# Ring slots, one-hot buffers and row counts in the expert stage of a diffusion trunk step

## What is computed

```python
q = einsum('btd,dhk->bthk', h, w_query).reshape(B, T, 8, 2, 128)
s = einsum('bthpk,hpnk->bthpn', q, sub_keys)     # 128 scores for each of two half keys
sv, si = top_k(s, 16)
best, pos = top_k(all 256 sums of a pair, 16)    # 16 of 16384 experts for each head
gates = softmax(best)
act = gelu(einsum('nd,ned->ne', h, expert_u[idx]))
out = einsum('ne,ned->nd', act * gates, expert_v[idx])
x = x + gt2 * out ; y = rmsnorm(x, norm_final)
```

## Time and profile before

| | |
|---|---|
| median of 3 runs | 5057.17 us (5048.15 to 5059.45) |
| the profiled execution, whole | 5038.0 us |
| its span in the trace | 5036.2 us |
| PE busy | 4752.4 us, 94% of the span |
| DVE busy | 3017.1 us, 60% |
| POOL busy | 1775.7 us, 35% |
| ACT busy | 579.1 us, 11% |
| mean granted clock of PE, as a share of full speed | 0.968 |
| read from HBM | 1643.31 MB, 330 GB/s over the span |
| the four stretches of the expert stage | from 3224.15 to 5023.83 us in the trace |

### The profile page before, as it was taken

The page is one execution under the profiler, slowest core; times in us unless marked ns, Lnnn a source line. Parts: engine busy times, 40 slices in busy tenths (PEclk is TensorE's granted clock), DMA queues, the critical chain, the costliest instruction groups (busy, mean ns, idle before and its releaser), DMA issues.

```text
span 5036.2 us, 54841 instructions
## 1 busy us (share of the span) xinstructions
PE 4752.4 (94%) x22501; PEld 3559.3 (71%) x22501; DVE 3017.1 (60%) x4381; ACT 579.1 (11%) x1078; POOL 1775.7 (35%) x1113
## 2 busy tenths in 40 slices
PE   4989999998999999899999999999999989999998
PEld 1787446445999444347555445799999988998898
DVE  1441006897766777317777578878855457776444
ACT  1521001441222100000000001100000000000000
POOL 0131001674555565211544353333432333332221
PEclk7999999999999999999999999999999999999999
DMA  9919898995221998996999987599999998999997
GB/s 389 380 51 351 314 342 323 386 392 233 76 89 68 371 396 342 414 352 255 420 420 420 376 346 294 205 372 406 409 407 405 397 381 346 353 347 363 377 366 302
DMA packets 262301, 1666.68 MB, mean 331 GB/s; under 512 B 28274, under 2 KB 32770, under 8 KB 78660
## 3 DMA queue, kind: packets, MB, share of 16 engines
q0 software_dynamic: 130048, 939.72, 46.7%
q1 hardware_dynamic: 123460, 673.84, 34.8%
q10 hardware_dynamic: 8544, 49.62, 2.5%
HBM read 1643.31 MB, written 18.94 MB: 330 GB/s over the span
## 4 chain that ended last, share of the span: by engine, by line
PE 33%; DMA 13%; DVE 7%; issue 2%; POOL 1%; ACT 0%; ACTq 0%; DVEq 0%; POOLq 0%
PE ps L241 14%; PE ps L2296 11%; DMA arena_sb<-peer_u,arena_sb 7%; DMA arena_sb<-peer_v 5%; PE ps L1720 4%; PE ps L2239 2%; DMA arena_sb<-peer_v,arena_sb 2%; DVE arena_sb L400 2%; DVE arena_sb L395 1%; DVE arena_sb L2486 1%; POOL arena_sb L349 0%; DVE arena_sb L2002 0%; DVE arena_sb L2012 0%; DVE arena_sb L2004 0%; DVE arena_sb L1999 0%
## 5 line engine op out<-in xcount | busy, mean ns | idle before, releaser
L241 PE MATMUL ps<-arena_sb 128*128 128x224 f32 (+3 forms) x9728 | 2317.9, 399 | 5.7 <-PEq L552 3.7
L241 PEld LDWEIGHTS ps<-arena_sb 128*128 128x128 f32 x9728 | 1692.8, 194 | 624.7 <-issue 336.4
L400 DVE SCALAR_TENSOR_TENSOR arena_sb<-arena_sb 128x2048 f32<-128x2048 f32 x412 | 985.8, 2393 | 397.7 <-DMA arena_sb<-peer_v,arena_sb 378.9
L395 DVE CUSTOM_DVE_ANT_0 arena_sb<-arena_sb 128x2048 f32<-128x2048 f32 x416 | 962.0, 2332 | 302.7 <-DMA arena_sb<-peer_u,arena_sb 302.5
L349 POOL DMA_INDIRECT arena_sb<-peer_v,arena_sb x416 | 688.3, 1655 | 1097.3 <-DVE arena_sb L400 579.0
L349 POOL DMA_INDIRECT arena_sb<-peer_u,arena_sb x416 | 654.8, 1574 | 851.1 <-DVE arena_sb L395 403.5
L2296 PE MATMUL ps<-arena_sb 128*128 128x224 f32 x4096 | 790.0, 355 | 33.7 <-DMA arena_sb<-peer_v 32.3
L2296 PEld LDWEIGHTS ps<-arena_sb 128*128 128x128 f32 x4096 | 776.8, 191 | 45.9 <-DMA arena_sb<-peer_v 42.4
L1570 PE MATMUL ps<-arena_sb 128*128 128x512 f32 x768 | 343.1, 605 | 20.9 <-PEq L2603 7.8
L1570 PEld LDWEIGHTS ps<-arena_sb 128*128 128x128 f32 x768 | 146.0, 193 | 213.4 <-issue 195.8
L1720 PE MATMUL ps<-arena_sb 128*128 128x512 f32 x640 | 277.9, 596 | 16.1 <-DVE arena_sb L1501 12.3
(11 more groups left out here) (279 smaller groups left out, 2919.7 us busy)
## 6 DMA issues: line engine op xcount, KB each, us to landing
arena_sb<-peer_ut SPq DMA_DIRECT2D x128, 1024.0 KB
arena_sb<-peer_v SPq DMA_DIRECT2D x128, 1024.0 KB
arena_sb<-w_mod POOLq DMA_DIRECT2D x64, 1024.0 KB, 9.0
arena_sb<-w_qkv SPq DMA_DIRECT2D x48, 1024.0 KB
arena_sb<-w_out SPq DMA_DIRECT2D x48, 1024.0 KB
arena_sb<-w_query SPq DMA_DIRECT2D x48, 1024.0 KB
arena_sb<-w_mod SPq DMA_DIRECT2D x32, 1024.0 KB
arena_sb<-w_ga_r SPq DMA_DIRECT2D x32, 1024.0 KB
```

The source lines that it names most:

```text
L241: mm = pe.matmul(out, weights[:, k * P:(k + 1) * P], x[:, k, :], start=(k == 0), stop=(k == chunks - 1))
L395: nc.vector.tensor_tensor_reduce(rows, rows, total, 1.0, 0.0, ALU.mult, ALU.add, seg.dots[:, p:p + 1]).then_inc(t.rows_used, 1)
L400: nc.vector.scalar_tensor_tensor(out=total, in0=rows, scalar=seg.weight[:, p:p + 1], in1=total, op0=ALU.mult, op1=ALU.add).then_inc(t.rows ...
```

## The change

Five edits in `experts`:

1. The second one-hot buffer moves from the scratch area to columns of `r.h2t` that the dense way doesn't read (tokens 224 and up), and both buffers are now used in both halves (`i = g % 2`).
2. In u1 `hot` stands two tiles ahead of its matmuls instead of one, and in both halves it stands before `use_rows` of its tile instead of after. In u1 the first `hot` also waits until all v tiles of half 0 are done, since `ring[3]` holds one of them.
3. `ring[3]` takes v tiles: a table `slot_of` cycles through slots 3, 1, 2, 0 in v0 and 3, 2, 0, 1 in v1, and through three slots in u0 and u1. A load waits until the tile before it in its slot is done. The first v load of a half also waits for the last group of gate matmuls.
4. `counts` moves row steps. By the two lists u0 has 100 instead of 98, v0 83 instead of 89, u1 122 instead of 112, and v1 has what remains of 374: 69 instead of 75. The first row step stands at tile 7 instead of 8.
5. x of the second segment no longer lies in `ring[3]` but shares a buffer with the first, so its load and what follows from it come some tiles later (tile 12 instead of 9 for `combine(1)`). The loads of `gt` and `norm` wait for the last gate matmuls, since they now overwrite the second one-hot buffer.

```diff
-    full = [t.sem(f"ex_full{i}") for i in range(3)]
+    full = [t.sem(f"ex_full{i}") for i in range(4)]
...
-    hots = ring[3], t.m[:, C + 8192:C + 8192 + TILE]
-    weighted = [ap[:, 0:TOKENS * P].rearrange("p (u n) -> p u n", u=TOKENS) for ap in hots]
-    plain = [ap[:, TOKENS * P:TOKENS * (P + HALF)].rearrange("p (u n) -> p u n", u=TOKENS) for ap in hots]
+    weighted = [ring[3][:, 0:TOKENS * P].rearrange("p (u n) -> p u n", u=TOKENS),
+                r.h2t[:, 0:TOKENS, DENSE:DENSE + P]]
+    plain = [ring[3][:, TOKENS * P:TOKENS * (P + HALF)].rearrange("p (u n) -> p u n", u=TOKENS),
+             r.h2t[:, TOKENS:2 * TOKENS, DENSE:DENSE + HALF]]
...
-    x = [t.m[:, DD + 2 * D:DD + 3 * D], ring[3], t.m[:, DD + 2 * D:DD + 3 * D], lead.total, spare.total]
+    x = [t.m[:, DD + 2 * D:DD + 3 * D], t.m[:, DD + 2 * D:DD + 3 * D], t.m[:, DD + 2 * D:DD + 3 * D], lead.total, spare.total]
...
+    slot_of, fill, before, last_in, fills = [], [], [], [None] * 4, [0] * 4
+    for cycle in ((0, 1, 2), (3, 1, 2, 0), (1, 2, 0), (3, 2, 0, 1)):
+        for i in range(HALF):
+            s = cycle[i % len(cycle)]
+            fills[s] += 1
+            slot_of.append(s)
+            fill.append(fills[s])
+            before.append(last_in[s])
+            last_in[s] = len(slot_of) - 1
...
-    hot_after = [{}, {s - 1: [g] for s, g in group_at[1].items()}]
-    for g, s in enumerate(starts[0]):
-        hot_after[0].setdefault(max(s - 2, starts[0][0] - 1), []).append(g)
+    hot_after = [{}, {}]
+    for h in range(2):
+        for g, s in enumerate(starts[h]):
+            hot_after[h].setdefault(max(s - 2, starts[h][0] - 1), []).append(g)
...
-    counts = [0] * 8 + [2, 2, 2, 1] * 14 + [1, 2, 1, 1, 2] * 12 + [1, 2, 1, 1] + [2, 1, 2, 2] * 16 + [1] + [1, 2, 1, 1] * 15
+    counts = [0] * 7 + [2, 2, 2, 1] * 14 + [2] + [1, 1, 2, 1, 1, 2, 1, 1, 2, 1] * 6 + [1, 1, 2, 1] + [2, 2, 2, 2, 2, 2, 2, 2, 2, 1] * 6 + [2] * 4 + [1, 1, 1, 1, 2] * 12
...
-            else:
-                sp.wait_ge(tile, n - 2)
+            elif before[n] is not None:
+                sp.wait_ge(tile, before[n] + 1)
+            if n % (2 * HALF) == HALF:
+                sp.wait_ge(gate_ps, GROUPS * (n // (2 * HALF) + 1))
...
-            n, i = GROUPS * h + g, 0 if h else g % 2
-            if h:
-                dve.wait_ge(gate_ps, n)
-            elif n > 1:
+            n, i = GROUPS * h + g, g % 2
+            if h and g == 0:
+                dve.wait_ge(tile, 2 * HALF)
+            if n > 1:
                 dve.wait_ge(gate_ps, n - 1)
...
                 gate(h, s)
-                use_rows(dve, nc, t, behind[2 * HALF * h + s])
                 for g in hot_after[h].get(s, ()):
                     hot(h, g)
+                use_rows(dve, nc, t, behind[2 * HALF * h + s])
```

More of the change, by code:

```diff
@@ L2184, in _ @@
                 sp.wait_ge(t.tile_done, base - 3 + n)
-            else:
-                sp.wait_ge(tile, n - 2)
+            elif before[n] is not None:
+                sp.wait_ge(tile, before[n] + 1)
+            if n % (2 * HALF) == HALF:
+                sp.wait_ge(gate_ps, GROUPS * (n // (2 * HALF) + 1))
             h, v = n // (2 * HALF), n % HALF
             if n // HALF % 2 == 0:
-                sp.dma_start(ring[n % 3], a["peer_ut"][HALF * h + v]).then_inc(full[n % 3], 16)
+                sp.dma_start(ring[slot_of[n]], a["peer_ut"][HALF * h + v]).then_inc(full[slot_of[n]], 16)
             else:
@@ L2193, in _ @@
                 low = (HALF * h + u * v) * P
-                sp.dma_start(ring[n % 3].rearrange("p (u n) -> p u n", u=u),
+                sp.dma_start(ring[slot_of[n]].rearrange("p (u n) -> p u n", u=u),
                              a["peer_v"][low:low + u * P, c * P:(c + w) * P]
-                             .rearrange("(u p) n -> p u n", u=u)).then_inc(full[n % 3], 16)
+                             .rearrange("(u p) n -> p u n", u=u)).then_inc(full[slot_of[n]], 16)
         for i, (out, n) in enumerate(dense):
@@ L2216, in loaded @@
         def loaded(n):
-            pe.wait_ge(full[n % 3], 16 * (n // 3 + 1))
+            pe.wait_ge(full[slot_of[n]], 16 * fill[n])
         def turn_keys():
@@ L2295, in add_rows @@
                         col = (s % u * w + i) * P
-                        mm = pe.matmul(t.ps[:, bank_of[h][first + i], 0:DENSE], ring[(n - 1) % 3][:, col:col + P],
+                        mm = pe.matmul(t.ps[:, bank_of[h][first + i], 0:DENSE], ring[slot_of[n - 1]][:, col:col + P],
                                        acts[:, s, :], start=(s == 0 and h == 0), stop=(s == HALF - 1))
@@ L2314, in _ @@
                 loaded(n)
-                project(pe, t.ps[:, u_banks[h][s % 2], 0:DENSE], ring[n % 3], h2t).then_inc(tile, 1)
+                project(pe, t.ps[:, u_banks[h][s % 2], 0:DENSE], ring[slot_of[n]], h2t).then_inc(tile, 1)
                 if h == 0 and s == starts[0][0] - 2:
@@ L2427, in _ @@
             if h:
+                act.wait_ge(gate_ps, 2 * GROUPS)
                 act.wait_ge(t.x_spilled, 16 * (2 * NB - 1))
@@ L2431, in _ @@
                 load_x(0)
-                act.wait_ge(gate_ps, 2 * GROUPS)
-                load_x(1)
             for s in range(HALF):
@@ L2437, in _ @@
                 if h:
[L2438 to L2443, removed]
+                    if s in (5, 12):
+                        square(s // 12)
+                    if s in (7, 14):
+                        store(s // 14)
+                    if s in (6, 13):
+                        load_x(1 + s // 13)
                     if s == 15:
@@ L2551, in _ @@
                 if h:
[L2552 to L2555, removed]
+                    if s in (5, 12):
+                        combine(s // 12)
+                    if s in (6, 13):
+                        scale(s // 13)
                     if s == 54:
```

## The result

| | kernel before | changed kernel |
|---|---|---|
| median of 4 runs | 5052.66 us | 4969.61 us (4955.71 to 4971.03) |
| ratio, 95% interval | 1 | 0.9835 (0.9802 to 0.9868) |
| span of the profiled execution | 5036.2 us | 4967.6 us |

The gain is 83 us where 86 were forecast. The windows of the changed kernel show where it lies. The columns are those of the earlier trace rows, and so are the stretches: u0, v0, u1, and v1 in two parts.

What follows compares the result with a forecast made beforehand. PE was taken to be held by waits for DVE's one-hot matrices in u1, with its lower clock, and for v tiles in v0 and v1. Gains 5 + 54 + 10 + 17 = 86 us off 5057.17 gave 4971 us, range 4948 to 5015.

Steps and rivals of the forecast that it cites:

- u1: the work of DVE ahead of PE: u1: PE waits for one-hot matrices behind DVE's row steps; 77.3 us lost, 35.5 in waits, 41.8 at PE's lower level.
- The floor: u1 without waits: 64 tiles with 28 groups are 437.3 us, plus one sum of 5.5 us, 442.8 us.
- u1: DMA becomes the limit: u1: 195.0 MB make DMA the new limit; 464 us at 420 GB/s, 483 at 404; taken as 466, gain 54.
- The first rival: u1: DMA gives what is asked, up to 440 GB/s; u1 443 to 455 us, kernel 4945 to 4960; chance 0.12.
- the fourth (354 GB/s): u1: DMA already at its limit of 354 GB/s; u1 551 us, kernel 5056, no change; chance 0.03.
- u1: "the first wait stays": Start of u1: PE's first wait, 7.74 us, stays, since group 0 has ten row steps ahead of it before and now.
- The second rival: u1: late gathers hold DVE and the next `hot`, the clock stays lower; kernel 4988 to 5025; chance 0.27.
- v0: the step that failed: v0: 147 blocks at 401 GB/s are 384 us, below PE's 389.8, so PE bounds; 394 us, gain 10.
- v1: the term that was mis-sized: v1: fewer row steps and a fourth slot shorten the two long waits; gain 17 us, bounds 6 and 26.
- u0: u0: `hot` ahead of row steps removes one wait of 2.54 us and its slow matmuls; gain 5, bound 0 to 8.
- The third rival: u0 and u1: row steps behind `hot` free slots 2.9 us later and starve the queues; kernel at 5136; chance 0.05.
- The sum: Whole kernel: 5 + 54 + 10 + 17 = 86 us off the median, 4971 us.

Runs made afterwards that it cites:

- half tiles: Changed kernel loading only the first half of the columns of each u tile of half 1, output no longer the reference's: 4940.3 us in one run.
- rows first: Changed kernel with `use_rows` moved back ahead of `hot`, still two tiles ahead: 4987.87 us, ratio 0.9875.

## Why the prediction was right, and where it was not

**u1: the work of DVE ahead of PE.** Right. With edits 1 and 2 alone all the loss goes, waits and slow clock together. The floor was set 1.8 us too high: the row of 5.51 us in the earlier trace rows stands behind a wait, at the lower clock, and in a u1 without waits this sum adds 3.7 us to a pair of tiles. So u1 lost 79 us, not 77.3.

**u1: DMA becomes the limit.** Right, and the main term of the sum: 461.8 us against 466. Its two rates were 404 and 420 GB/s; the trace shows 413 at a share of 1.00. The two kernels that change only bytes settle it: 6 steps more cost 14 us, and half the tile bytes bring the floor. The first rival (440 GB/s) and the fourth (354 GB/s) fall with it. That 466 came so near is partly luck: all 195.0 MB at 413 GB/s would take 472 us, and u1 was shorter because it left part of its bytes to v1, which the sum didn't have. By the Trainium skill's rule of about 358 GB/s (page "DMA: Bandwidth & Descriptors", section "Where 436 GB/s comes from") u1 would have taken 545 us; no stretch with full queues here was as slow as that.

**u1: "the first wait stays".** Right for the changed kernel (7.30 us for my 7.74), but my reason was short. I counted ten row steps ahead of the first group before and after. With the old counts and the new order it is nine, since `hot` now stands ahead of the row steps of tile 5, and the wait is gone in one execution and 2.83 us in the other. With nine row steps and the new sum (one row step moved) it is 1.15. So most of this wait belongs to edit 4.

**The second rival**, that DVE stays late and the clock low with it, has its waits in the second half of u1, of 0.2 to 1.5 us. They cost little: PE was idle for 14.9 us in u1 (forecast 15) and busy for 446.9 against 441.1 in a clean one. Its price was reckoned loosely: a sum of 64 gives 4993 us, not 4988, as the first rival's 443 us give a gain of 109, not 112.

**v0: the step that failed.** The size was near (13.4 us for 10), the cause was not. "147 blocks at 401 GB/s are 384 us, so PE is the bound by a little" took the rate of a stretch that waits for the rate that the queues can give. The fourth slot alone gives 391.2 us with 153 blocks, and 147 blocks with three slots give 402.9. What three slots can't cover is the time of one transfer. With three slots the load of tile n is issued when tile n - 3 is done, two tiles or 12.2 us ahead of need; with four it is 18.3 us. The view of one tile gives the time from issue to landing of the v tiles of v0, first with three slots (edits 1 and 2 alone), then with four (the fourth slot alone), both with 153 blocks:

```profile
DMA to landing us min/median/max: 6.8/11.3/15.4
```

```profile
DMA to landing us min/median/max: 10.7/13.3/19.8
```

Load by load, 21 of the 64 with three slots take more than 12.2 us, and each of PE's 17 waits in v0 ends with the landing of one that took 12.3 to 15.2 us. With four slots PE waits twice, for loads of 19.0 and 19.8 us.

**v1: the term that was mis-sized.** 7.5 us instead of 17. The fourth slot alone gave 17.3 (427.9 to 410.6). The changed kernel lost 10 of that again, and what fits is that u1 at its DMA limit hands on what it has not moved: 413 GB/s in 461.75 us are 190.7 MB of the 195.0 that belong to u1. POOL had issued 118 of the 122 gathers in u1, against 121 of 122 with half tiles and 111 of 112 with the old counts. The three kernels whose u1 ran into the limit with 122 or 128 row steps (413 to 415 GB/s) had 219 to 223 us in the first part of v1; where the changed counts met little backlog (half tiles; rows first, at 405 GB/s) it was 209.7 and 212.5. This is a comparison of kernels that differ in other things too, so the cause is argued and not shown. Edit 4 took six row steps from v1, and v1 was no shorter for it.

**u0.** Right in size, 4.9 us for 5. Hot behind the row steps costs 12.5 us there, so the order counts for more than the one wait that I read in the earlier trace rows.

**The third rival**, that the new order starves the queues, is refuted by its opposite: the old order with two tiles of lead is slower in both u stretches and moves bytes no faster.

**The sum** was right in part because errors cancel: v0 was 3 and u1 4 us better than forecast, and v1 9.5 us worse. What it missed is that edit 4, which its terms for v0 and v1 count as a gain, has a cost: without it the kernel gains 106 and 110 us in two comparisons, instead of 83.

## What to carry to other kernels

On an engine that works in order, put work that another engine waits for ahead of work that only has to be done some time, and give it a buffer and a lead so that it covers more than one step of the consumer. A rate that a stretch shows while its consumer waits is no capacity: compare with another depth of buffering before bytes are moved out of it. Before optional work is moved into a stretch that has just been freed of waits, set its bytes per time against the highest rate that any stretch shows; here 112 row steps just fitted and 122 did not. And before an experiment is read, see in its trace whether the edit moved what it was to move: here three loads written at later tiles were issued when they always were.

## What the runs showed of the hardware

In the kernel before, 14 of the 15 waits of u1 were of 1.7 to 2.2 us, most of them followed by groups of 2.6 to 3.7 us instead of 1.89, and u1 ran at 0.92. PE was busy there for 484.6 us against 441.1 in a u1 without waits. So most of the 79 us was not waiting but slow matmuls, 43 against 35.5 us.

The length of a wait alone doesn't say whether the clock falls behind it. In u1 of the changed kernel nine short waits, up to 1.54 us, left it alone: the two tiles behind that one take 12.33 us, as in a clean pair. In the kernel with one row step moved, the two tiles behind a wait of 0.95 us take 14.01, and the granted clock from that wait to the next group is 0.89. Behind a wait of 2.37 us later in the same u1 they take 12.32, at 1.00:

```profile
4353.01 2.00 PE L2252 MATMUL ps<-arena_sb 128*128 128x64 f32 x16 [0.95 <-DVE arena_sb L2500]
4354.85 14.01 PE L241 MATMUL ps<-arena_sb 128*128 128x224 f32 x64
```

```profile
4427.75 2.00 PE L2252 MATMUL ps<-arena_sb 128*128 128x64 f32 x16 [2.37 <-DVE arena_sb L2500]
4429.59 12.32 PE L241 MATMUL ps<-arena_sb 128*128 128x224 f32 x64
```

What decides it is not shown. In u1 of the kernel before, the way from a group behind a wait to the end of the next two tiles took 15.7 or 17.3 us instead of 13.9, so a slow stretch cost 1.8 or 3.4 us beside its wait.

v tiles read as rows of 4 KB (17249 packets for 67.44 MB in the queue of the tile loads), with gathers of 8 KB rows beside them, ran at 414 GB/s in v0 of the changed kernel with the old counts, the same as tiles of 8 KB rows in its u1. With three slots the same blocks moved at 400 and 401 GB/s.
